# Modulation weights laid out by contraction rows and multiplied on four column groups

## The chip, the cores and the metric

The kernel runs on one core of one Trainium2 chip. The metric is the device time of one execution in microseconds (us). The inputs are float32 throughout, and every matmul is a float32 matmul, which the trace records as two entries (one matmul of 256 moving columns shows as "x2").

## The reference, cut to what matters

One layer of a decoder runs on 256 prompt tokens and 8 sample rows (one new token for each of 8 sequences), at width 1024. The change touches only the modulation: six vectors of 1024 for the prompt and for each of the 8 samples.

```
def adaln(c, w_ada, b_ada):
    m = jax.nn.silu(c) @ w_ada + b_ada
    return [t[:, None, :] for t in jnp.split(m, 6, axis=-1)]

sh1, sc1, g1, sh2, sc2, g2 = adaln(c, w_ada[layer], b_ada[layer])     # for the prompt and for the samples
h  = rms_norm(x, norm_mix) * (1.0 + sc1) + sh1
qa, ka, va, qb, kb, vb = project_qkv(h, w_in, pos)    # 8 stick-breaking heads, 8 dilated window heads
x  = x + g1 * merge_out(oa, ob, norm_out_sb, norm_out_dil, w_out)
h2 = rms_norm(x, norm_ffn) * (1.0 + sc2) + sh2
x  = x + g2 * peer_ffn(h2, ...)                       # 16 of 16384 experts for each of 8 heads
y  = rms_norm(x, norm_final)
```

`w_ada` is 1024 x 6144, `c` has 9 rows (8 samples and the prompt). The samples also attend to 2048 past tokens: paged K and V caches for the stick-breaking heads (16 pages of 128 tokens each), window buffers for the dilated heads. The outputs hold the new K/V rows and whole copies of the window buffers, shifted by one row.

## The kernel before, in words

The kernel is written by hand, engine by engine: each engine has its own program in a fixed order, and semaphores tie them together. Nothing is scheduled automatically. All tiles live in SBUF for the whole run.

Weights come in 48 chunks of 1 MB, four in a round, into four slots (`W`, slots 0 to 3 of `R`). A chunk is 256 output columns of a weight matrix for all 1024 contraction rows, 8 KB on each of 128 partitions. GpSimd (POOL) issues them: the load of a slot's next chunk waits until TensorE (PE) has counted the slot as used (`w_used`). Rounds 0 and 1 are the first two modulation vectors (shift 1, scale 1), rounds 2 to 4 the q/k/v projection, rounds 5 to 8 the other four vectors, round 9 the output projection, rounds 10 and 11 the PEER queries.

The program passes through these stages:

1. Front. `c` is put through silu as 9 rows of 1024 (L815, L1099 to L1101), turned by PE (L461) into `cT`, and multiplied with 8 chunks (`ada_chunk`, L472: eight matmuls with 9 stationary columns and 256 moving columns, then a ninth, L474, that adds the bias by a one-hot selector that ScalarE (ACT) makes, L821). ACT evicts 9x256 pieces to `m_rows` (L827). VectorE (DVE) folds the norm's gain in (L1126), PE spreads the prompt's row over 128 partitions (L481), ACT evicts it to `m_all` (L842), and DVE modulates the three token tiles (L1116, L1117).
2. Projection. PE multiplies 12 chunks (`project`, L510). After the first four it spreads the samples' queries (L532), ACT evicts them, and from there DVE works through the K pages of samples 0 to 3 (`page_scores`: a multiply, L1140, and a reduction, L1142, for each chunk of two pages) beside PE's other eight chunks.
3. Sticks. Four rounds g of a loop, a pair of heads and a sample (4 to 7) each. DVE's order in a round: L1158, K chunks 0 and 1, L1164 and L1166, chunks 2 and 3, L1170, chunks 4 and 5, L1174, chunks 6 and 7, L1177. PE answers between: transposes (L543), scores (L553, L554), sums (L561 to L564), values (L574 to L576), and beside them `ada_chunk` for slots 0 and 1 behind the scores and for slots 2 and 3 behind the sums.
4. V pages of the 8 samples on PE (L594) beside the dilated heads; then the gate's spread (L481) and the V windows of the dilated heads (L699).
5. Output projection (L510), second modulation, PEER queries (L744), and then 264 gathers of expert rows of 1 MB each (L432) with a dot product on DVE and a product on PE for each.

SyncE (SP) issues the other loads in one fixed order. Small inputs come first; then it waits for them (`small_in`) and issues the first 8 K pages (L285); then 24 pieces of 1 MB of the window copies (L296), each held until the piece before it of the same kind has landed; then the K pages of the rest of sample 0 and of samples 1 to 7, each held until DVE has used its slot; then output rows, V pages with some copy pieces between, the V windows (L261, L262: four DMAs for a sample), and the last copies.

Of the kernel before, what the change touches and what calls it, by code (L numbers as in the profile page):

```python
# [15 lines left out]
ALU = mybir.AluOpType  # L16
# [23 lines left out]
NKEY = 128  # L40
NSLOT = 8
# [8 lines left out]
GATE1, SHIFT2, SCALE2, GATE2 = range(4)  # L50
EPS = 1e-6
# [73 lines left out]
def build(nc, A):  # L125
    ctx = ExitStack()
    with ctx:
# [14 lines left out]
        m_rows = sb("m_rows", [9, 4, D])  # L142
# [7 lines left out]
        nffn = sb("nffn", [9, D])  # L150
        b24 = sb("b24", [ADA_CH, WC])
        zd = sb("zd", [P, 3, NB * NH])
        zrow = sb("zrow", [NB * NH, 384])
        pd = sb("pd", [P, 3, NB * NH])
        cT = sb("cT", [P, KC, 9])
        bsel = sb("bsel", [ADA_CH, 2, 9])
# [15 lines left out]
        diag = sb("diag", [P, 4, P])  # L172

# [14 lines left out]
        cwork = [Z[0:9, n, :] for n in range(3)]  # L188
# [15 lines left out]
        def row_slot(k):  # L204
# [18 lines left out]
        names = """c9_in c_in x_in small_in w_used sel_ready ada_mm ada_ev bc_mm bc_ev cs_ready cT_mm cT_ev m1_ready  # L223
# [6 lines left out]
          kst dst sbs dis tks subk_in z_v topsm tope fin_in""".split()  # L230
# [17 lines left out]
        def wait_apart(eng, semaphore, value):  # L248


            if not isinstance(value, int):
                eng.reg_mov(wait_value[eng], value)
                value = wait_value[eng]
            eng.wait_ge(s["c_in"], 48)
            eng.wait_ge(semaphore, value)
# [11 lines left out]
        def _(sp):  # L267
            sp.dma_start(cwork[0], A["c9"]).then_inc(s["c9_in"], 16)
            sp.dma_start(const[:, :], A["consts"]).then_inc(s["c_in"], 16)
            sp.dma_start(cwork[2], A["norm_mix"].to_broadcast([9, D])).then_inc(s["c_in"], 16)  # L270
            sp.dma_start(b24[:, :], A["b_ada"]).then_inc(s["c_in"], 16)
            for t in range(3):
                sp.dma_start(x[0:TP[t], t, :], A["x"][t * P:t * P + TP[t], :]).then_inc(s["x_in"], 16)
            sp.dma_start(nffn[:, :], A["norm_ffn"].to_broadcast([9, D])).then_inc(s["small_in"], 16)
# [3 lines left out]
            sp.wait_ge(s["small_in"], 64)  # L278
# [63 lines left out]

            sp.wait_ge(s["new_out"], 32)
# [109 lines left out]
        def _(pe):  # L453
# [4 lines left out]
            pe.wait_ge(s["c_in"], 48)  # L458
            pe.wait_ge(s["cs_ready"], 1)
            for c in range(KC):  # L460
                last = pe.transpose(ps[:, 7, c * 9:(c + 1) * 9], cwork[0][:, c * P:(c + 1) * P], ident[0:9, 0:9])  # L461
            last.then_inc(s["cT_mm"], 1)
            pe.wait_ge(s["cT_ev"], 1)

            def ada_chunk(r, first, sel, k, bank):

                w_round(r + first, k)

                pe.wait_ge(s["sel_ready"], (r + sel) * WSLOTS + (k + 1))
                out = ps[0:9, bank + k % 2, 0:WC]  # L470
                for c in range(KC):
# [1076 lines left out]
```

## Times and profile before

| | us |
|---|---|
| median of 3 runs | 1369.17 (1368.55 to 1369.77) |
| span of the profiled execution | 1367.5 |
| PE busy in it | 1121.9 (82%) |
| DVE busy | 790.2 (58%) |
| ACT busy | 374.5 (27%) |
| POOL busy | 389.7 (28%) |
| DMA, over the span | 479.79 MB, mean 351 GB/s |

The profiled execution is told by its span, from the first instruction to the last; the median of the unprofiled runs is 1.7 us above it. Busy shares are averages over stages with different limits, so what counts for an edit is the stage that it stands in and which engine or transfer is the last to be ready there. The profile's chain of waits follows the work back from the last instruction, and its waits view says for whom each engine sat idle.

### The profile page before, as it was taken

Reading aid. Unit: us, or ns where it says so; the run is one execution under the profiler, and the core shown is the slowest. Engines: PE = TensorE matmul, PEld = TensorE weight load, DVE = VectorE, ACT = ScalarE, POOL = GpSimd, SP = SyncE. Lnnn points to the kernel's source line nnn. Section 1 sums busy time; section 2 is a strip of 40 time slices with the busy share of each in tenths; the row PEclk is TensorE's granted clock in tenths of the full one; section 3 lists DMA queues with packets and bytes.
Section 4 is the critical chain, followed back from the end, with each engine's and each line's share of the span. In section 5 each row is a group of like instructions: output and inputs, shape, how many; then the busy total and the mean of one; then the engine's idle time right before and its main releaser. Section 6 shows DMA issues by size and latency. Waiting matters only on the chain.

```text
span 1367.5 us, 14726 instructions
## 1 busy us (share of the span) xinstructions
PE 1121.9 (82%) x3386; PEld 503.3 (37%) x3386; DVE 790.2 (58%) x1679; ACT 374.5 (27%) x1030; POOL 389.7 (28%) x384
## 2 busy tenths in 40 slices
PE   6799998998787888998997778777768777777875
PEld 2375774443221211457852323233223333232321
DVE  4203996976512411324437777777777677777755
ACT  1201004434110000002233333333344334444323
POOL 1000003020201000000125555555535555555540
PEclk9898999996999997998999999999999999999998
DMA  9998887898698886899659999999999999999995
GB/s 335 426 358 303 298 312 270 323 356 301 220 284 252 251 269 215 322 390 339 232 207 423 422 422 422 422 422 422 422 421 379 422 422 422 422 422 422 422 422 221
DMA packets 91422, 479.79 MB, mean 351 GB/s; under 512 B 11792, under 2 KB 11817, under 8 KB 50172
## 3 DMA queue, kind: packets, MB, share of 16 engines
q0 software_dynamic: 46912, 332.47, 60.3%
q1 hardware_dynamic: 44476, 146.92, 30.9%
q8 instruction: 15, 0.25, 0.1%
q14 instruction: 19, 0.16, 0.0%
HBM read 476.10 MB, written 70.32 MB: 400 GB/s over the span
## 4 chain that ended last, share of the span: by engine, by line
PE 37%; DMA 32%; issue 10%; DVE 8%; SPq 6%; ACT 4%; POOL 2%; POOLq 0%; DVEq 0%; ACTq 0%
DMA R<-in_uv,idst 26%; PE ps L510 13%; PE ps L791 8%; PE ps L744 4%; SPq L284 3%; DMA R<-in_sb_v 3%; PE ps L472 3%; SPq L285 2%; DVE R L1140 2%; PE ps L699 2%; PE ps L594 2%; POOL R L432 2%; DMA R<-in_sb_k 2%; PE ps L481 1%; ACT wgt L1050 1%
## 5 line engine op out<-in xcount | busy, mean ns | idle before, releaser
L791 PE MATMUL ps<-R,diag 128*128 128x512 f32 x1024 | 482.1, 619 | 153.4 <-ACT diag L1069 153.4
L432 POOL DMA_INDIRECT R<-in_uv,idst x256 | 320.9, 1254 | 332.5 <-PE ps L791 260.4
L1454 DVE CUSTOM_DVE_ANT_0 R<-R,H 128x1024 f32<-128x1024 f32 x264 | 318.6, 1222 | 162.7 <-DMA R<-in_uv,idst 152.3
L791 PEld LDWEIGHTS ps<-R,diag 128*128 128x128 f32 x1024 | 192.4, 196 | 443.1 <-ACT diag L1069 241.6
L510 PE MATMUL ps<-R,HT 128*128 128x256 f32 (+1 forms) x768 | 172.7, 384 | 1.0 <-DVE HT L1335 0.4
L378 POOL DMA_DIRECT2D R<-in_wts x44 | 23.4, 531 | 508.9 <-PE ps L510 341.9
L594 PE MATMUL ps<-R,ast 128*8 128x512 f32 x256 | 123.0, 625 | 27.6 <-DMA R<-in_sb_v 24.0
L510 PEld LDWEIGHTS ps<-R,HT 128*128 128x128 f32 (+1 forms) x768 | 119.0, 158 | 55.3 <-issue 12.1
L1047 ACT ACTIVATE gel<-dots 128x2 f32<-128x2 f32 x132 | 26.8, 203 | 377.3 <-DVE dots L1454 377.3
L1140 DVE TENSOR_TENSOR R<-R 128x1024 f32<-128x1024 f32 x64 | 78.2, 1221 | 66.2 <-ACT R L874 57.6
L472 PE MATMUL ps<-R,cT 128*9 128x256 f32 x384 | 92.8, 398 | 1.3 <-ACT bsel L821 1.3
L1069 ACT ACTIVATE diag<-const,wgt 128x128 f32<-128x128 f32 x256 | 89.1, 394 | 16.1 <-PE ps L791 3.2
L1142 DVE TENSOR_REDUCE Z<-R 128x1024 f32 x64 | 78.1, 1220 | 9.1 <-DVE R L1140 0.2
L1258 DVE TENSOR_TENSOR msk<-ps,const 8x512 f32<-8x512 f32 x16 | 10.9, 679 | 97.4 <-PE ps L594 57.5
L594 PEld LDWEIGHTS ps<-R,ast 128*8 128x8 f32 x256 | 20.8, 92 | 119.6 <-issue 67.9
L1050 ACT ACTIVATE wgt<-gel,gst 128x1 f32<-128x1 f32 x264 | 63.3, 287 | 4.3
L744 PE MATMUL ps<-HT,R 128*128 128x264 f32 x256 | 59.9, 393 | 0.3 <-ACT HT L855 0.3
L472 PEld LDWEIGHTS ps<-R,cT 128*9 128x9 f32 x384 | 34.3, 94 | 55.8 <-issue 14.8
L744 PEld LDWEIGHTS ps<-HT,R 128*128 128x128 f32 x256 | 49.0, 194 | 8.6 <-ACT HT L855 0.4
L863 ACT ACTIVATE QKV<-ps 128x512 f32 (+1 forms) x12 | 7.2, 598 | 120.9 <-PE ps L510 120.9
L261 POOL DMA_DIRECT2D m_all<-in_dil_k x24 | 12.9, 538 | 95.6 <-DVE zd L1223 95.0
L699 PE MATMUL ps<-R,ast 128*8 128x512 f32 (+2 forms) x48 | 29.8, 775 | 7.9 <-DMA R<-out_dil_v_s 5.8
(233 smaller groups left out, 872.3 us busy)
## 6 DMA issues: line engine op xcount, KB each, us to landing
R<-in_wts POOLq DMA_DIRECT2D x48, 1024.0 KB, 8.1
R<-in_sb_k SPq DMA_DIRECT2D x128, 256.0 KB, 4.4
R<-in_sb_v SPq DMA_DIRECT2D x128, 256.0 KB, 3.4
out_dil_k_s<-in_dil_k SPq DMA_DIRECT2D x32, 1023.5 KB, 8.0
out_dil_v_s<-in_dil_v SPq DMA_DIRECT2D x32, 1023.5 KB, 7.9
R<-in_uv,idst POOLq DMA_INDIRECT x256, 12.1
m_all<-in_dil_k POOLq DMA_DIRECT2D x16, 192.0 KB, 6.1
R<-in_dil_v SPq DMA_DIRECT2D x16, 192.0 KB
```

The source lines that it names most:

```text
L432: pool.indirect_dma_start(out=R[:, row_slot(k), :], out_offset=None, in_=A["uv"], in_offset=bass.IndirectOffsetOnAxis(ap=idst[:, par, k:k ...
L472: last = pe.matmul(out, cT[:, c, :], W[k][:, c, :], start=(c == 0), stop=False)
L510: last = pe.matmul(out, hT[:, c, t * P:t * P + TP[t]], W[k][:, c, :], start=(c == 0), stop=(c == KC - 1))
L594: last = pe.matmul(ps[0:NH, 6 + j, :], ast[:, j, c * KVP + g, :], KV[c % KVS][:, g, :], start=(c + g == 0), stop=(c * KVP + g == NPG - 1))
L699: last = pe.matmul(ps[0:NH, 6 + j, :], ast[0:n, j, g, :], DV[j][0:n, g, :], start=(g == 0), stop=(g == 2))
L744: last = pe.matmul(ps[:, j, 0:NTOK], W[k][:, c, j * P:(j + 1) * P], hT[:, c, :], start=(c == 0), stop=(c == KC - 1))
L791: last = pe.matmul(ps[:, banks + q, :], diag[:, k % 4, :], R[:, row_slot(k), D + q * 512:D + (q + 1) * 512], start=False, stop=False, skip ...
L1050: last = act.activation(wgt[:, k + q:k + q + 1], gel[:, k + q:k + q + 1], ACT.Copy, scale=gst[:, k + q:k + q + 1])
L1069: act.activation(diag[:, k % 4, :], ident, ACT.Copy, scale=wgt[:, k:k + 1]).then_inc(s["diag_done"], 1)
L1140: kc.inc(dve.tensor_tensor(kv, kv, q, ALU.mult))
L1142: dve.tensor_reduce(z4[:, c * KVP:(c + 1) * KVP, bass.ds(b, 1), :].rearrange("p g a h -> p g (a h)"), kv.rearrange("p g (h d) -> p g h d", ...
L1454: dve.tensor_tensor_reduce(u, u, H[:, t, :], 1.0, 0.0, ALU.mult, ALU.add, dots[:, k:k + 1]).then_inc(s["dot_done"], 1)
```

## The change

The modulation weights are laid out in another way in memory: a chunk now holds 256 of the 1024 contraction rows for one whole vector of 1024 columns (`pairs` in place of `chunks`), so a round of four chunks is one vector. A chunk is still 1 MB, 8 KB on each partition. PE multiplies a chunk with two contraction blocks and four column blocks of 256: the output of column block q goes to partitions 32q to 32q+8 of one PSUM bank, with 32 stationary columns (9 of `c` and 23 of zeros) on column group q of the array. `c` comes already turned (`cT`, 128 x 8 x 32). The bias matmul, its selector and ACT's evictions go. The bias, laid out on the same partitions (`mq`), is added by DVE as it evicts the bank (`ada_rows`). The samples' rows, which must be on partitions 0 to 7 for tile 2, are moved from `mq` to `m_rows` by DMAs of 8 x 1 KB: 8 from ACT's queue in the front, 16 from SP's in front of the V windows. The prompt's row is spread by matmuls over all 128 contraction rows, 256 columns at a time.

```diff
-            sp.dma_start(cwork[0], A["c9"]).then_inc(s["c9_in"], 16)
+            sp.dma_start(cT[:, :, :], A["cT"].rearrange("p (c n) -> p c n", c=KC)).then_inc(s["c9_in"], 16)
             sp.dma_start(const[:, :], A["consts"]).then_inc(s["c_in"], 16)
-            sp.dma_start(cwork[2], A["norm_mix"].to_broadcast([9, D])).then_inc(s["c_in"], 16)
-            sp.dma_start(b24[:, :], A["b_ada"]).then_inc(s["c_in"], 16)
             for t in range(3):
                 sp.dma_start(x[0:TP[t], t, :], A["x"][t * P:t * P + TP[t], :]).then_inc(s["x_in"], 16)
-            sp.dma_start(nffn[:, :], A["norm_ffn"].to_broadcast([9, D])).then_inc(s["small_in"], 16)
+            sp.wait_ge(s["mq_clear"], 1)
+            for k in range(QUADS):
+                q = slice(k * QUAD, k * QUAD + NB + 1)
+                cols = slice(k * WC, (k + 1) * WC)
+                sp.dma_start(mq[q, :, :], A["b_ada"][k:k + 1].to_broadcast([NB + 1, VECTORS, WC])).then_inc(s["mq_in"], 16)
+                sp.dma_start(nq[q, 0, :], A["norm_mix"][:, cols].to_broadcast([NB + 1, WC])).then_inc(s["mq_in"], 16)
+                sp.dma_start(nq[q, 1, :], A["norm_ffn"][:, cols].to_broadcast([NB + 1, WC])).then_inc(s["mq_in"], 16)
...
             value_pages(NB - 1)
 
+            sp.wait_ge(s["m2_ready"], 1)
+            for v, slot in LATE_VECTORS:
+                for k in range(QUADS):
+                    sp.dma_start(m_rows[:, slot, k * WC:(k + 1) * WC], mq[k * QUAD:k * QUAD + NB, v, :]).then_inc(s["mr_in"], 16)
             sp.wait_ge(s["new_out"], 32)
...
-            def ada_chunk(r, first, sel, k, bank):
-                w_round(r + first, k)
-                pe.wait_ge(s["sel_ready"], (r + sel) * WSLOTS + (k + 1))
-                out = ps[0:9, bank + k % 2, 0:WC]
-                for c in range(KC):
-                    last = pe.matmul(out, cT[:, c, :], W[k][:, c, :], start=(c == 0), stop=False)
-                last.then_inc(s["w_used"], 1)
-                pe.matmul(out, bsel[:, k % 2, :], b24[:, :], start=False, stop=True).then_inc(s["ada_mm"], 1)
+            def ada_slots(r, first, bank, slots):
+                for k in slots:
+                    w_round(r + first, k)
+                    for c in range(2):
+                        for q in range(QUADS):
+                            last = pe.matmul(ps[q * QUAD:(q + 1) * QUAD, bank, 0:WC], cT[:, 2 * k + c, :],
+                                             WA[k][:, c, q * WC:(q + 1) * WC], start=(k + c == 0), stop=(2 * k + c == KC - 1))
+                    last.then_inc(s["w_used"], 1)
...
-                for k in range(2):
-                    ada_chunk(g, 5, 2, k, 6)
+                if not first:
+                    pe.wait_ge(s["ada_ev"], g + 2)
+                ada_slots(g, 5, 6, (0, 1))
...
+            act.wait_ge(s["m1_ready"], 1)
+            for v, slot in FIRST_VECTORS:
+                for k in range(QUADS):
+                    act.dma_start(m_rows[:, slot, k * WC:(k + 1) * WC], mq[k * QUAD:k * QUAD + NB, v, :]).then_inc(s["mr_in"], 16)
...
+            dve.memset(mq[:, :, :], 0.0)
+            dve.memset(nq[:, :, :], 0.0).then_inc(s["mq_clear"], 1)
...
+            def ada_rows(v, bank, chunks_used):
+                dve.wait_ge(s["w_used"], chunks_used)
+                mv = mq[:, bass.ds(v, 1), :].rearrange("p a n -> p (a n)")
+                dve.tensor_tensor(mv, ps[:, bank, 0:WC], mv, ALU.add).then_inc(s["ada_ev"], 1)
...
                 page_scores(g + 4, (6, 7))
+                ada_rows(g + 2, 6, g * WSLOTS + (2 * WSLOTS + QKV_CH + WSLOTS))
                 dve.wait_ge(s["o_mm"], g + 1)
...
+    def pairs(w):
+        return w.reshape(WSLOTS, 2, P, -1, D).transpose(3, 0, 2, 1, 4).reshape(-1, P, 2 * D)
```

Three places show how the instructions stand. On PE, in the first round of the sticks stage, behind the second score matmul (`ps<-R,cT` are the modulation's, `ps<-b,bsel` the bias's), before:

```order
49 L554 MATMUL ps<-HT 128x128
50 L472 MATMUL ps<-R,cT 9x256 x8
51 L474 MATMUL ps<-b,bsel 9x256
52 L472 MATMUL ps<-R,cT 9x256 x8
53 L474 MATMUL ps<-b,bsel 9x256
54 L561 MATMUL ps<-H,const 128x128
```

The same place after:

```order
33 L566 MATMUL ps<-HT 128x128
34 L481 MATMUL ps<-R,cT 32x256 x16
35 L574 MATMUL ps<-H,const 128x128
```

Two chunks are 16 matmuls in both; their outputs are 32 partitions instead of 9, and the two bias matmuls between are gone. On DVE, at the end of a round of the sticks loop, behind the last K chunk, before and then after:

```order
104 L1142 ISA
105 L1142 TENSOR_REDUCE Z<-R 128x2x8
106 L1177 ISA
107 L1177 COPY QKV<-ps 128x2x128
108 L1155 REGISTER_ALU
```

```order
108 L1147 TENSOR_REDUCE Z<-R 128x2x8
109 L1100 ISA
110 L1102 ISA
111 L1102 TENSOR_TENSOR mq<-ps,mq 128x256
112 L1183 ISA
113 L1183 COPY QKV<-ps 128x2x128
```

One more operation, and the wait of L1100 for PE's four slots, stand in front of the copy of the values. On SP, between the last V page and the first V windows, before and then after:

```order
508 L285 DMA R<-in_sb_v 128x512
509 L261 DMA R<-in_dil_v 128x512
510 L261 DMA R<-in_dil_v 96x512 x2
511 L262 DMA R<-out_dil_v_s 1x512
```

```order
517 L295 DMA R<-in_sb_v 128x512
518 L356 DMA m_rows<-mq 8x256 x16
519 L267 DMA R<-in_dil_v 128x512
520 L267 DMA R<-in_dil_v 96x512 x2
521 L268 DMA R<-out_dil_v_s 1x512
```

Sixteen small DMAs now stand in front of the V windows of samples 0 and 1.

## Rows read from the trace of the kernel before

**Rows 1.** The page: the chain that ended last, by engine.
```profile
PE 37%; DMA 32%; issue 10%; DVE 8%; SPq 6%; ACT 4%; POOL 2%; POOLq 0%; DVEq 0%; ACTq 0%
```
**Rows 2.** Windows by stage: PE, PEld, DVE, ACT, POOL busy, granted clock, DMA share, GB/s.
```profile
0.00:122.50 122.50, 101.00 (x393) 52.72 (x393) 22.64 (x20) 20.60 (x47) 8.86 (x20) 0.90 0.97 372
122.50:214.30 91.80, 88.86 (x398) 61.40 (x398) 75.73 (x64) 10.49 (x23) 7.41 (x16) 0.98 0.85 286
214.30:320.00 105.70, 93.82 (x446) 45.37 (x446) 94.34 (x97) 37.85 (x70) 20.28 (x37) 0.89 0.91 325
```
**Rows 3.** Timeline of the front: start, us, engine, line.
```profile
14.13 5.09 PE L472 MATMUL ps<-R,cT 128*9 128x256 f32 x16 [0.60 <-ACT bsel L821]
27.83 3.62 PE L472 MATMUL ps<-R,cT 128*9 128x256 f32 x16
48.42 0.59 PE L474 MATMUL ps<-b,bsel 24*9 24x256 f32 x2
66.96 42.69 PE L510 MATMUL ps<-R,HT 128*128 128x256 f32 x192 [0.31 <-ACT HT L855]
```
**Rows 4.** SP's timeline: first K pages, last of 24 copies, next pages.
```profile
23.09 8.10 SPq L285 DMA_DIRECT2D R<-in_sb_k  x8
122.37 0.51 SPq L296 DMA_DIRECT2D out_dil_v_s<-in_dil_v  x1
126.88 183.68 SPq L285 DMA_DIRECT2D R<-in_sb_k  x120
```
**Rows 5.** DMA queues (packets, MB, share): 70 to 80 us, then 80 to 90 us.
```profile
q1 hardware_dynamic: 93, 3.01, 85.8%
...
q1 hardware_dynamic: 77, 2.23, 53.5%
q0 software_dynamic: 143, 1.05, 26.8%
```
**Rows 6.** DVE's timeline: first and fifth K chunk, last of sample 3, sticks begin.
```profile
123.52 1.22 DVE L1140 TENSOR_TENSOR R<-R 128x1024 f32<-128x1024 f32 x1 [57.60 <-ACT R L874]
133.51 1.21 DVE L1140 TENSOR_TENSOR R<-R 128x1024 f32<-128x1024 f32 x1
204.59 1.22 DVE L1142 TENSOR_REDUCE Z<-R 128x1024 f32 x1
214.35 1.14 DVE L1158 TENSOR_SCALAR H<-ps,sbb 128x384 f32<-128x384 f32 x2 [8.54 <-PE ps L554]
```
**Rows 7.** Waits of DVE, 215 to 320 us: us, times, longest.
```profile
DVE R L1140 <- DMA R<-in_sb_k: 6.5, 4, 3.2
```
**Rows 8.** DVE's timeline in a sticks round: an operation that reads PSUM.
```profile
264.84 0.41 DVE L1177 COPY QKV<-ps 128x256 f32 x1
```
**Rows 9.** PE's timeline at the sticks' start: scores on 64 rows.
```profile
213.24 0.71 PE L553 MATMUL ps<-HT 64*128 64x256 f32 x4 [1.19 <-ACT HT L887]
213.78 0.40 PE L554 MATMUL ps<-HT 64*128 64x128 f32 x4
```
**Rows 10.** Groups of weight loads: L472 from 0 to 70 us, L510 (page); busy, mean ns.
```profile
L472 PEld LDWEIGHTS ps<-R,cT 128*9 128x9 f32 x128 | 11.3, 93 | 19.6 <-issue 4.2 <-ACT bsel L821 2.3
...
L510 PEld LDWEIGHTS ps<-R,HT 128*128 128x128 f32 (+1 forms) x768 | 119.0, 158 | 55.3 <-issue 12.1
```
**Rows 11.** SP and PE at the V windows.
```profile
508.00 1.29 SPq L261 DMA_DIRECT2D R<-in_dil_v  x3
516.29 8.29 PE L699 MATMUL ps<-R,ast 128*8 128x512 f32 x12 [0.47 <-ACT selst L921]
523.35 0.23 SPq L262 DMA_DIRECT2D R<-out_dil_v_s  x1
526.12 2.74 PE L699 MATMUL ps<-R,ast 128*8 128x512 f32 x6 [0.58 <-DMA R<-out_dil_v_s]
```
**Rows 12.** SP's issue of one DMA, in ns (min/median/max): from memory, from 8 partitions.
```profile
L261 SPq DMA_DIRECT2D R<-in_dil_v x24: 317/352/556, 508.0 to 551.8; - x24
L324 SPq DMA_DIRECT2D out_sb_k_n<-QKV x1: 1452/1452/1452, 315.8 to 315.8; - x1
```

More of the change, by code:

```diff
@@ L40 @@
 NKEY = 128
+QUAD = 32
+QUADS = P // QUAD
+VECTORS = 6
+PROMPT = NB
 NSLOT = 8
@@ L186, in build @@
         z1, zt, zl = Z[:, 0, :], Z[:, 1, :], Z[:, 2, :]
-        cwork = [Z[0:9, n, :] for n in range(3)]
+        cwork = [Z[:, n, 0:KC * QUAD] for n in range(2)]
+        WA = [R[:, s, :].rearrange("p (c n) -> p c n", c=2) for s in range(WSLOTS)]
         Hf = H[:, :, :].rearrange("p t n -> p (t n)")
@@ L455, in w_round @@
                 pe.wait_ge(w_ready[k], r * 16 + 16)
[L458 removed]
+            pe.wait_ge(s["c_in"], 16)
             pe.wait_ge(s["cs_ready"], 1)
[L460 to L474 removed]
@@ L476, in spread_rows @@
-            def spread_rows(order, n, banks, mm, ev):
-                for m, slot in enumerate(q for q in order for _ in range(2)):
+            def ada_slots(r, first, bank, slots):
[6 more added lines that the diff above has]
+                    last.then_inc(s["w_used"], 1)
@@ L479, in spread_rows @@
+            def spread_rows(vectors, n, banks, mm, ev):
+                for m, v in enumerate(v for v, _ in vectors for _ in range(2)):
                     if m >= len(banks):
                         pe.wait_ge(ev, n + m - len(banks) + 1)
-                    pe.matmul(ps[:, banks[m % len(banks)], :], ident[0:9, 8:9].to_broadcast([9, P]),
-                              m_rows[:, slot, (m % 2) * 512:(m % 2 + 1) * 512], start=True, stop=True).then_inc(mm, 1)
+                    for j in range(2):
+                        k = 2 * (m % 2) + j
+                        last = pe.matmul(ps[:, banks[m % len(banks)], j * WC:(j + 1) * WC],
+                                         ident[:, k * QUAD + PROMPT:k * QUAD + PROMPT + 1].to_broadcast([P, P]),
+                                         mq[:, v, :], start=True, stop=True)
+                    last.then_inc(mm, 1)
@@ L513, in project @@
                         last.then_inc(s["w_used"], 1)
-            with pe.Fori(0, 2) as r:
-                for k in range(WSLOTS):
-                    ada_chunk(r, 0, 0, k, 0)
+            for r in range(2):
+                ada_slots(r, 0, r, range(WSLOTS))
             pe.wait_ge(s["m1_ready"], 1)
-            spread_rows((SHIFT1, SCALE1), 0, (4, 5, 6, 7), s["bc_mm"], s["bc_ev"])
+            spread_rows(FIRST_VECTORS, 0, (4, 5, 6, 7), s["bc_mm"], s["bc_ev"])
             pe.wait_ge(s["bc_ev"], 4)
@@ L565, in sticks_pair @@
                 last.then_inc(s["s_mm"], 1)
-                for k in range(2, 4):
-                    ada_chunk(g, 5, 2, k, 6)
+                ada_slots(g, 5, 6, (2, 3))
                 pe.wait_ge(s["s_am"], g + 1)
@@ L1529 @@
         "pages": a["page_table"].reshape(1, NB * NPG),
-        "wts": np.concatenate([chunks(w) for w in (a["w_ada"][0][:, :2 * D], a["w_in"][0], a["w_ada"][0][:, 2 * D:],
-                                                   a["w_out"][0], a["w_peer_q"][0])], 0),
+        "wts": np.concatenate([pairs(a["w_ada"][0][:, :2 * D]), chunks(a["w_in"][0]), pairs(a["w_ada"][0][:, 2 * D:]),
+                               chunks(a["w_out"][0]), chunks(a["w_peer_q"][0])], 0),
         "subk": a["peer_sub_keys"].reshape(16, NKEY, P).transpose(2, 0, 1).reshape(P, 16 * NKEY),
```

99 lines of the change are left out of this document (43 added, 56 removed).

## The prediction, made before the changed kernel was run

> **What bounds the kernel now.** I read the chain that ended last first [rows 1]: no engine holds it, PE has 37% of it and DMA 32%, so the kernel must be read by stages. The windows [rows 2] give three that the change touches. The front and the first chunks of the projection, up to 122.5 us, keep PE busy for 101.0 us with the DMA engines at a share of 0.97. From 122.5 to 214.3 us PE is busy for 88.9 of 91.8 us beside DVE's K pages of samples 0 to 3. In the sticks stage, 214.3 to 320.0 us, PE shows 93.8 us and DVE 94.3 us of 105.7: both look full, and only the waits tell which is last.
>
> They say this. In the sticks stage DVE waits for K pages, 6.5 us in all [rows 7], and in a list of what it waited for there PE does not stand. So DVE and its pages set that stage, and PE's modulation matmuls lie beside it. One wait for PE stands just ahead of it: DVE ends sample 3's pages at 204.59 + 1.22 = 205.8 us and then idles 8.54 us until the first scores, at 214.35 us [rows 6], because PE is still in the projection. And SP shows a limit that the chain hides [rows 4]: the 24 copy pieces end at 122.37 + 0.51 = 122.9 us, and only behind them come the pages from the fifth chunk on, at 126.88 us, 3.1 us after DVE began at 123.52 us. Before the change that limit is just covered.
>
> **The front.** The eight modulation chunks run from 14.13 us to 48.42 + 0.59 = 49.0 us [rows 3], 34.9 us. A chunk is 16 entries in 3.62 us less the overlap of the last, 0.222 us each, the first at half clock. A chunk of the new layout has the same 16 entries of 256 columns. If four column groups ran fully side by side, a chunk would take 0.9 us; PE would then wait for the weights. The trace shows tiles overlapping only for row groups: two score matmuls of 256 columns and two of 128, on 64 rows each, run from 213.24 to 214.18 us [rows 9], 0.94 us, where one after the other at 0.222 us for an entry of 256 columns they need 2 x 0.44 + 2 x 0.22 = 1.33 us. I take it that column groups overlap as well, and that the chunks then come at the pace of their loads: the second four MB are asked for by about 18 us instead of 20 to 32 us, and at some 0.35 MB per us beside the K pages they are in by about 30 to 33 us. That is 16 to 19 us earlier than 49.0; the two evictions on DVE stand for ACT's last one. The bounds are 34.9 - 28.4 = 6.5 us (no overlap: 128 entries x 0.222 = 28.4 us) and about 20 us. The silu is on 256 elements a partition rather than 1024, and the 8 DMAs on ACT's queue stand ahead of its evictions; both fall into the same term. The projection, 192 entries in 42.69 us for its first four chunks [rows 3], keeps its length, so the first scores, at 213.24 us now [rows 9], could stand about 17 us earlier, near 196 us.
>
> **What is late next.** DVE's pages of samples 0 to 3 could start near 106 us, but their fifth chunk cannot: SP still has copies to issue. How far do these move? Copies alone run at 3.0 MB in 10 us, and at 2.2 MB beside 1.05 MB of weights [rows 5]: one MB of weights costs them 0.8 MB, some 2.6 us. With PE 17 us ahead, 1 to 2 more chunks (one for 10.65 us) fall into their time: +2.5 to 5 us. The front's DMA is denser earlier, -2. The first K pages stand behind 12 small DMAs more, +0 to 2. I take +2.5, so the copies are issued by 125.4 us. The fifth chunk needs two pages to be issued (about 1 us each, 8 in 8.10 us [rows 4]) and some 5 us to land: 132.4 us, against 133.51 us before [rows 6]. DVE's last page of sample 3 then ends at 204.7 us and, since PE is ready at 196 us, the sticks begin there: 214.35 - 204.8 = 9.5 us earlier. The front's large term is cut to this, the idle 8.54 us and 1 us more. PE's other 8 us gained end as waiting for DVE. Bounds of this term: 12.5 us (copies not later) and 3.5 us (copies and landings 6 us later still).
>
> **The sticks stage.** Removed from PE are four chunks of 4.1 us (3.55 us and a bias matmul) of its 93.82 / 4 = 23.5 us a round, 16.3 us; put in at a quarter to seven eighths of that: worth nothing, as DVE is last there. Added on DVE are four evictions of 128x256 with an addition, each like the copy of 256 columns from PSUM, 0.41 us [rows 8]: 4 x 0.4 = +1.6 us. Behind each stand the copy of the values and the next round's first operation, for which ACT and PE wait in turn. The added wait on `w_used` is over long before: the slots of a round are multiplied behind L561 to L564, 13 us ahead of it. PE will be idle more and may run at the half level of the clock; the granted clock fell to 0.89 of full over this stage already [rows 2]. Between DVE's last mask (L1174) and its next L1158 lie two K chunks (32 in 82.3 us [rows 6], 2.6 us each) and the copy, 5.5 us, in which PE and ACT must do values, transposes and scores; at half clock I estimate 6 for them, so up to 0.5 us for each of three rounds and a little at the end: +1 us, between 0 and 3. The waits for pages, 6.5 us [rows 7], can move: weights are asked for in pairs at once, but 2 MB of them ahead of the stage. I keep them at 6.5, between 0 and 10.
>
> **The V windows.** SP issues 16 small DMAs ahead of the windows. The price of one issue is 0.35 us for loads from memory and was 1.45 us for one from 8 partitions of SBUF [rows 12], which stood in a stretch where SP's other issues were slow too. I take 0.35: 5.6 us, and keep 16 x 1.45 = 23.2 us as the other end. Sample 0's windows are four issues (1.29 us for three, 1.9 in all) and landed within 2.5 us of the last where the queue was empty: 523.35 + 0.23 to 526.12 us [rows 11]. Moved by 5.6 us they are there at 508.0 + 5.6 + 1.9 + 2.5 = 518.0 us, and PE wanted them at 516.29 us: +2 us (bounds 0 and 19). The later windows wait for PE's use and follow it. The last copies start later by the same, but end 50 us ahead of the gathers. The gate's spread is the same number of columns, in twice the entries of half the width: 0.
>
> **The sum.** -9.5 + 1.6 + 1 + 2 = -4.9 us. Everything behind is tied to these stages by waits and moves with them, the gathers at their pace. The span of 1367.5 becomes 1362.6; the median of the runs lies 1.7 us above the span, so 1369.2 - 4.9 = 1364.3 us.
>
> The Trainium skill speaks against the layout at one place: by "TensorE: Matmul & The Clock Gate", Part 3 (packing small matmuls), a weight load overlaps a running matmul only where their row groups differ, and here all four column groups use all rows. This trace doesn't agree for full-width matmuls: entries with loads of 93 ns and entries with loads of up to 190 ns (158 ns in the mean) [rows 10] both follow each other at 0.222 us (192 in 42.69 us [rows 3]), so the load is hidden. The same part gives 2.38 times for three column tiles, which would make the front's PE work about 12 us, an estimate by that page; the loads cover it either way.
>
> **The rivals.**
> - No overlap of column groups. For it: no row shows it for columns. Against: the row groups. PE ends 6.5 us earlier, the sticks start at 207.9 us: -6.5 + 1.6 + 2 = -2.9, 1366.3 us.
> - No overlap and the weight loads in the open. An entry costs 0.222 + 0.093 = 0.315 us, the front 40.3 us (+5.4), a sticks round 64 x 0.315 + 7.2 = 27.4 us of PE against 26.4 (+4), windows +2: 1380 us. It is the page's rule as a mechanism; rows 10 speak against it.
> - The small DMAs in front of the V windows (the slower side). At 1.45 us an issue the windows are there at 508.0 + 23.2 + 1.9 + 2.5 = 535.6 us, +19.3 instead of +2: 1381.6 us. It eats the whole gain where an issue costs over 0.65 us (16 t = 6.9 + 8.3 - 4.4 = 10.8 us).
> - The copies hold DVE. If the fifth chunk comes at 138.5 us, the sticks begin near 210.9 us: -3.5 + 4.6 = +1, 1370.3 us: the front's gain is hidden anyway.
> - The copies aren't later, or the page waits of the sticks go: -3 or -6.5 more, near 1358 us.
>
> **How the numbers follow.** Forecast 0.47, with a range of its own of 1361 to 1367; no overlap 0.12; loads in the open 0.04; slow small issues 0.10; copies hold DVE 0.15; better 0.12. A change of 0.2% (2.7 us) is about what a measurement of this kernel can tell from none. Faster by more: nearly all of the forecast, half of no overlap, all of better: 0.62. Within: 0.22. Slower: slow issues, loads in the open, and the bad part of the copies: 0.16. The range is 1357 to 1371: it takes in the better case and the copies, and leaves out the two cases near 1380.
>
> **What would show it.** The first L523 starts near 48 us (66.96 before); copies are issued by 125 us; the fifth K chunk at 132 us with a wait for its page; the wait of 8.54 us for PE is gone and the first score evictions stand near 205 us; PE idle in the sticks stage, DVE not; the first V window matmul waits for its DMA, 2 us late. I am wrong if the sticks begin later than 208 us, if they take over 110 us, or if the windows start over 5 us late against the last V page.

## The result

The kernel after takes 1381.89 us in the median of 18 runs (1371.33 to 1388.60), the kernel before 1370.29 us in 18 runs on the same chips (1363.34 to 1378.38). The ratio is 1.0082 (95% interval 1.0061 to 1.0102): the change makes the kernel slower by 11.6 us, where 4.9 us faster was forecast. The profiled execution has a span of 1380.5 us against 1367.5, 13.0 us more.

### The profile page after: what moved, and what is told of

It reads as the page before. It is cut to its first block, busy times and chain, and to the rows that moved or that the text cites. A ratio compares the mean times of both kernels' runs of the same rounds, so it can differ in the third digit from the quotient of the medians.

```text
span 1380.5 us, 14581 instructions
## 1 busy us (share of the span) xinstructions
PE 1057.9 (77%) x3354; PEld 495.3 (36%) x3354; DVE 788.1 (57%) x1687; ACT 363.4 (26%) x979; POOL 396.1 (29%) x384
## 4 chain that ended last, share of the span: by engine, by line
DMA 42%; PE 24%; issue 11%; SPq 9%; DVE 7%; ACT 4%; POOL 2%; POOLq 0%; DVEq 0%; ACTq 0%
DMA R<-in_uv,idst 25%; PE ps L803 8%; DMA out_dil_v_s<-in_dil_v 6%; DMA R<-in_sb_k 5%; PE ps L756 4%; SPq L294 4%; PE ps L606 3%; PE ps L523 3%; SPq L295 3%; DMA R<-in_sb_v 2%; POOL R L446 2%; DVE R L1145 2%; DMA pages<-in_pages 2%; PE ps L711 1%; DVE R L1460 1%
## 5 line engine op out<-in xcount | busy, mean ns | idle before, releaser
L446 POOL DMA_INDIRECT R<-in_uv,idst x256 | 325.4, 1271 | 328.5 <-PE ps L803 256.7
L1061 ACT ACTIVATE diag<-const,wgt 128x128 f32<-128x128 f32 x256 | 89.5, 395 | 17.1 <-PE ps L803 4.2
L481 PE MATMUL ps<-R,cT 128*32 128x256 f32 x384 | 36.4, 534 | 24.0 <-DMA R<-in_wts 21.6
L574 PE MATMUL ps<-H,const 128*128 128x128 f32 x16 | 5.7, 461 | 38.9 <-DVE H L1171 38.9
## 6 DMA issues: line engine op xcount, KB each, us to landing
R<-in_uv,idst POOLq DMA_INDIRECT x256, 12.2
```

Source lines behind the costliest of these rows:

```text
L446: pool.indirect_dma_start(out=R[:, row_slot(k), :], out_offset=None, in_=A["uv"], in_offset=bass.IndirectOffsetOnAxis(ap=idst[:, par, k:k ...
L1061: act.activation(diag[:, k % 4, :], ident, ACT.Copy, scale=wgt[:, k:k + 1]).then_inc(s["diag_done"], 1)
```

## The profile after

The chain that ended last, by engine, answers [rows 1]: DMA has 42% of it instead of 32%, PE 24% instead of 37%.

```profile
DMA 42%; PE 24%; issue 11%; SPq 9%; DVE 7%; ACT 4%; POOL 2%; POOLq 0%; DVEq 0%; ACTq 0%
```

The three stages that answer [rows 2] (the same columns: us, then PE, PEld, DVE, ACT, POOL busy, granted clock, DMA share, GB/s):

```profile
0.00:112.00 112.00, 80.31 (x378) 47.64 (x379) 18.58 (x24) 16.03 (x29) 8.89 (x20) 0.91 0.96 355
112.00:219.40 107.40, 89.69 (x428) 61.51 (x426) 77.29 (x64) 9.95 (x23) 17.87 (x30) 0.93 0.86 301
219.40:327.40 108.00, 55.35 (x384) 39.85 (x384) 95.14 (x101) 31.17 (x38) 11.65 (x22) 0.64 0.91 321
```

The front is 10 us shorter than before, the second stage 15.6 us longer, and the third 2.3 us longer though PE is busy in it for 55.35 us instead of 93.82. So PE lost work, and the time went into something else. PE's timeline of the front, against [rows 3]:

```profile
10.94 1.93 PE L481 MATMUL ps<-R,cT 128*32 128x256 f32 x16 [10.94 <-DMA R<-in_wts]
...
35.11 1.57 PE L481 MATMUL ps<-R,cT 128*32 128x256 f32 x16 [0.48 <-DMA R<-in_wts]
37.70 3.72 PE L492 MATMUL ps<-mq,const 128*128 128x256 f32 x16 [1.02 <-DVE mq L1133]
...
54.51 15.81 PE L523 MATMUL ps<-R,HT 128*128 128x256 f32 x58 [0.31 <-ACT HT L852]
```

All eight modulation chunks wait for their weights, each takes 1.93 us (the last 1.57 us) instead of 3.62, and the last ends at 35.11 + 1.57 = 36.7 us instead of 49.0: 12.3 us earlier. (The first four loads take until 23.77 us to land, so POOL asks for the last of the second four at 26.39 us.) The projection starts at 54.51 us instead of 66.96, 12.5 us earlier. Between the two stands ACT, which issues 8 small DMAs before its first eviction (ACTq is ACT's queue):

```profile
37.68 5.88 ACTq L841 DMA_DIRECT2D m_rows<-mq  x8
43.60 2.06 ACT L835 ACTIVATE m_all<-ps 128x512 f32<-128x512 f32 x4 [23.12 <-issue]
```

SP's timeline answers [rows 4], and DVE's [rows 6]:

```profile
8.88 0.28 SPq L287 DMA_DIRECT2D pages<-in_pages  x1
34.38 8.12 SPq L295 DMA_DIRECT2D R<-in_sb_k  x8
42.55 0.66 SPq L306 DMA_DIRECT2D out_dil_k_s<-in_dil_k  x1
```

```profile
134.56 0.51 SPq L306 DMA_DIRECT2D out_dil_v_s<-in_dil_v  x1
135.89 14.12 SPq L295 DMA_DIRECT2D R<-in_sb_k  x9
```

```profile
112.38 1.23 DVE L1145 TENSOR_TENSOR R<-R 128x1024 f32<-128x1024 f32 x1 [59.26 <-ACT R L871]
...
121.24 1.22 DVE L1147 TENSOR_REDUCE Z<-R 128x1024 f32 x1
146.22 1.23 DVE L1145 TENSOR_TENSOR R<-R 128x1024 f32<-128x1024 f32 x1 [23.76 <-DMA R<-in_sb_k]
...
219.41 1.14 DVE L1163 TENSOR_SCALAR H<-ps,sbb 128x384 f32<-128x384 f32 x2
```

DVE begins 11.1 us earlier (112.38 us against 123.52), works through the four chunks that it has, and then idles 23.76 us for the fifth, which comes at 146.22 us instead of 133.51. SP could not issue it: the 24 copy pieces end 12.2 us later than before. The sticks start at 219.41 us, 5.1 us later instead of 9.5 us earlier. The wait of 8.54 us for PE ahead of them is gone. PE starts its first scores at 201.84 us, against 213.24 us [rows 9]: 11.4 us of its gain arrive here, and DVE is not ready to use them.

```profile
201.84 0.71 PE L565 MATMUL ps<-HT 64*128 64x256 f32 x4 [1.19 <-ACT HT L884]
```

The DMA queues show what stands behind the late copies (packets, MB, share of the 16 engines; q0 carries the weights, q1 is SP's). First the kernel after from 20 to 30 us, then from 30 to 40, then from 50 to 60:

```profile
q0 software_dynamic: 431, 3.14, 94.4%
q1 hardware_dynamic: 280, 0.17, 7.3%
```

```profile
q0 software_dynamic: 536, 3.88, 93.8%
q1 hardware_dynamic: 207, 0.26, 7.2%
```

```profile
q1 hardware_dynamic: 151, 3.80, 99.9%
```

Before, from 30 to 40 us:

```profile
q1 hardware_dynamic: 810, 3.40, 84.6%
q0 software_dynamic: 182, 1.35, 32.2%
```

The new layout uses a slot in 1.93 us, so POOL asks for weights nearly as fast as they land, and up to 40 us they take most of the engines' time. In the ten microseconds from 30 us SP's queue moved 0.26 MB, against 3.40 MB before. This is not contention alone: SP still waited for the page table and issued its first K page at 34.38 us. Then PE's slow chunks of the projection (10.65 us each) ask for little: from 37.9 to 68.6 us POOL issues no weight chunk, and from 50 to 70 us the copies run nearly alone.

Two things can be counted. By the issue of the 24th copy, at 122.37 us, the kernel before had moved 45.5 MB, 28.75 of them on SP's queue and 16.77 of weights: 372 GB/s. The kernel after had moved 47.0 MB (29.10 and 17.81) at 134.56 us: 350 GB/s. So 1.5 MB more stood ahead of that point, mostly one more weight chunk, and the pace was lower. At the pace before, the 1.5 MB are some 4 us (an estimate from these numbers), and the lower pace is the other 8 of the 12.2 us. The lower pace stands mostly in one stretch: the totals up to 30 us and from 70 to 120 us differ by under 0.2 MB each, from 30 to 70 us the two queues moved 17.1 MB before and 14.8 MB after.

In the sticks stage DVE's waits answer [rows 7] (us, times, longest):

```profile
DVE R L1145 <- DMA R<-in_sb_k: 7.4, 6, 2.5
DVE H L1163 <- PE ps L566: 0.7, 1, 0.7
```

The stage lasts from 219.41 to 327.40 us, 108.0 us against 105.6: four `ada_rows` at 0.416 us, 0.9 us more waiting for pages, 0.7 us for PE. One profile doesn't fix such a difference: the same stage took 107.9 to 113.1 us in the kernels below with this layout, and 111.4 us in the second run of e7's kernel, which has the old one. In front of the V windows, against [rows 11], SP and then PE:

```profile
520.77 10.89 SPq L356 DMA_DIRECT2D m_rows<-mq  x16
531.78 1.31 SPq L267 DMA_DIRECT2D R<-in_dil_v  x3
```

```profile
524.82 1.99 PE L492 MATMUL ps<-mq,const 128*128 128x256 f32 x8
...
536.53 7.70 PE L711 MATMUL ps<-R,ast 128*8 128x512 f32 x12 [8.77 <-DMA R<-out_dil_v_s]
```

The 16 small DMAs take 10.89 us, 0.68 us each. The first window matmul comes 11.7 us behind the gate's spread (524.82 to 536.53), before it came 3.5 us behind it (512.79 to 516.29): +8.2 us.

The 13.0 us by stages: start of the sticks +5.1; sticks +2.4; from there to the gate's spread +4.6; windows' start +8.2; and then -3.7 to the merge, -2.0 to the second modulation, -1.8 to the first gathered dot product, +0.3 behind it. The +4.6 can't be put down to the layout: in the kernels below with this layout, that stretch lasts between 190.6 and 199.6 us, and in three profiles with the old one 192.8 (before), 193.3 and 195.9 us.

## The experiments

e1 to e4 ran on one chip, e6 to e9 on a second and e10 to e12 on a third, each time beside the kernel before (1372.02, 1372.73 and 1371.72 us there). Where runs from two chips are compared, the ratios to the kernel before count.

Two theories stood for the late copies. One: the page table (`pages`) is issued behind 12 small loads, at 8.88 us instead of 5.31, so SP reads it late and everything behind it slips. The other: weights asked for earlier take the transfer engines from the copies, wherever the page table stands.

**The small loads first (e1_small_first).**

```diff
+            sp.dma_start(sbb...); sp.dma_start(gcol...); sp.dma_start(pages...)      # small_in
             sp.wait_ge(s["mq_clear"], 1)
             for k in range(QUADS):
                 ...                                                                  # the 12 loads of mq and nq
-            sp.dma_start(sbb...); sp.dma_start(gcol...); sp.dma_start(pages...)
             sp.wait_ge(s["small_in"], 48)
```

> The changed kernel with SP's three last small loads (stick bias, output gain, page table) issued ahead of the 12 small loads of biases and norm gains instead of behind them. Theory (late page table: K pages, copies and with them the fifth K chunk are late because the page table's load lands at 33.4 us behind the 12 new small loads): SP's first K page near 22 us instead of 34.4, last copy issued near 124 us instead of 134.6, fifth K chunk near 135 us instead of 146.2, time about 11 us under the changed kernel, ratio to the kernel before near 1.000. Rival (the copies are late because earlier weight loads take their bandwidth, wherever they start): last copy issued after 130 us, time within 4 us of the changed kernel.

1382.87 us (5 runs), ratio 1.008 (1.0048 to 1.0111): as slow as the kernel after. SP's timeline, and DVE's:

```profile
25.86 8.14 SPq L295 DMA_DIRECT2D R<-in_sb_k  x8
34.06 0.66 SPq L306 DMA_DIRECT2D out_dil_k_s<-in_dil_k  x1
```

```profile
131.97 0.51 SPq L306 DMA_DIRECT2D out_dil_v_s<-in_dil_v  x1
```

```profile
141.17 1.23 DVE L1145 TENSOR_TENSOR R<-R 128x1024 f32<-128x1024 f32 x1 [16.85 <-DMA R<-in_sb_k]
```

SP's first pages and copies come 8.5 us earlier than in the kernel after, the last of the 24 only 2.6 us. The copies now take 98 us instead of 92. The fifth chunk comes 5 us earlier, but later pages are waited for more, and the sticks start at 218.51 us, 0.9 us earlier. The first theory falls as an explanation of the time; it is true only of when the copies start. (This profile is of the slowest of the five executions.)

**The page table before the second round of weights (e4_hold_weights).**

```diff
+            pool.wait_ge(s["small_in"], 48)
             weight_rounds(1, 6)
```

> The changed kernel with POOL's second round of modulation weights held until the small loads have landed. Theory A (small packets are slow on SP's queue because POOL's queue always has 8 KB packets beside them): page table landed by about 24 us instead of 33.4, copies issued by 126 us, time 7 to 10 us under the changed kernel although the modulation ends some 6 us later. Theory B (the 12 small loads take their time by themselves): page table still after 30 us, time within 3 us of the changed kernel.

1385.21 us (4 runs), ratio 1.0094 (1.0062 to 1.0125). Its SP:

```profile
26.65 8.09 SPq L295 DMA_DIRECT2D R<-in_sb_k  x8
```

```profile
133.11 0.51 SPq L306 DMA_DIRECT2D out_dil_v_s<-in_dil_v  x1
```

The page table is read 7.7 us earlier with nothing moved on SP, so the weights beside it had held it up. The 24th copy still goes out at 133.11 us, and DVE's first chunk is later too (121.18 us, 112.38 in the kernel after). The expected gain of 7 to 10 us did not come. A start of the copies some 8 us earlier moved their end by 2.6 us in e1 and by 1.4 us here, and the pace up to the 24th copy was 349 and 346 GB/s, no higher than in the kernel after.

**The 16 row DMAs behind the windows (e2_rows_late), and both moves (e3_both).**

```diff
-            sp.wait_ge(s["m2_ready"], 1)
-            for v, slot in LATE_VECTORS: ...                 # 16 DMAs mq -> m_rows
             ...
             for b in range(2):
                 window_rows(sp, DV, b, b, A["dil_v"], A["dil_v_s"], dv_ready)
+            sp.wait_ge(s["m2_ready"], 1)
+            for v, slot in LATE_VECTORS: ...
```

> The changed kernel with the 16 small DMAs of the sample rows moved on SP from in front of the V windows of samples 0 and 1 to behind them, where SP waits for PE anyway. Theory (the issue of 16 DMAs, 10.9 us, holds the V windows): the first window matmul stands 3 to 4 us behind the gate's spread instead of 11.7 us, time about 8 us under the changed kernel, ratio near 1.002. Rival (the windows would be late anyway, by their own landing): first window matmul still over 8 us behind, time within 3 us of the changed kernel.

1378.01 us (10 runs), ratio 1.0042 (1.0014 to 1.0071). PE at the windows:

```profile
521.48 1.99 PE L492 MATMUL ps<-mq,const 128*128 128x256 f32 x8
...
524.89 5.33 PE L711 MATMUL ps<-R,ast 128*8 128x512 f32 x12 [0.47 <-ACT selst L913]
```

The wait of 8.77 us for the windows is gone, and 3.4 us lie between the spread and the first window matmul, as before. The next two samples' windows now stand behind the 16 DMAs and PE waits 5.23 us for them, so a part of the 8.3 us is given back: the ratio falls by 0.4%, some 5 us (the two intervals just overlap).

> Both moves at once. If the two causes are separate and all of the loss, the gains add: some 19 us under the changed kernel, ratio to the kernel before near 0.995. If the second K-page stall or PE's lower clock in the sticks stage is a cause of its own, the ratio stays at 1.000 or above.

1377.73 us, ratio 1.0052 (1.0027 to 1.0078): the small loads add nothing to e2, as e1 says, and the 19 us that I expected of both moves came to about 4. The copies end at 135.04 us and the fifth chunk comes at 146.35. It is the base of the next three.

**Eight copy pieces out of the front (e6_copies_later).** On top of e3:

```diff
                     copy_windows(0, 0)
                     copy_windows(0, 1)
-                    copy_windows(1, 0)
...
-                        copy_piece(2, 0, c // 4, q)          # beside the V pages
+                        copy_piece(1, 0, c // 4, q)
...
-            for pair, odd in ((2, 1), (3, 0), (3, 1)):       # at the end
+            for pair, odd in ((2, 0), (2, 1), (3, 0), (3, 1)):
```

> The kernel of e3 (small loads first, sample rows late) with 8 of the 24 copy pieces moved out of the front: sample 2's pieces take the places among the V pages, sample 4's go to the end with the last copies. Theory (the copies in front of the fifth K chunk are the place where the front's gain is lost): the last of 16 pieces is issued near 100 us, DVE's wait at the fifth chunk shrinks from 21.8 us to under 3 us, sticks end near 312 us instead of 329, time about 15 us under e3, ratio to the kernel before near 0.992. Rival (DMA bandwidth as a whole holds the K pages of the first three stages, whoever asks first): the wait is spread over the later K pages, sticks end above 322 us, ratio above 1.000.

1364.84 us, ratio 0.9945 (0.9918 to 0.9972): 1.1% below e3's ratio, some 14 us, and faster than the kernel before. SP, then the end of DVE's pages of sample 3 and its start of the sticks:

```profile
102.02 0.51 SPq L306 DMA_DIRECT2D out_dil_v_s<-in_dil_v  x1
117.72 6.40 SPq L295 DMA_DIRECT2D R<-in_sb_k  x6
```

```profile
195.71 1.22 DVE L1146 TENSOR_REDUCE Z<-R 128x1024 f32 x1
206.45 1.14 DVE L1162 TENSOR_SCALAR H<-ps,sbb 128x384 f32<-128x384 f32 x2 [9.51 <-PE ps L565]
```

The last of 16 pieces goes out at 102.02 us. The next K pages are held until 117.72 us by DVE's own use of the slots. No wait for a page in the projection is over 1.1 us, and the sticks start at 206.45 us behind a wait of 9.51 us for PE. So the copies were what held DVE. That 206.45 us lies near the 204.8 us of the prediction is in part luck: there PE was ready at 196 us and DVE's pages ended last, at 204.7 us; here DVE's pages end at 196.9 us and PE is last, with its first scores at 204.61 us. The sticks end at 314.9 us, near the 312 expected and far from the rival's 322.

**The same move in the kernel before (e7_before_copies_later).** Its diff is the one above, on the kernel before.

> The kernel before, with the same 8 copy pieces moved out of the front and nothing else. Theory (before the change PE's projection covers the copies, so they cost nothing there): first K chunk still at 123.5 us, sticks end within 4 us of 320 us, ratio 0.997 to 1.003. Rival (the copies cost the kernel before as much): sticks end below 312 us, ratio under 0.993.

1367.42 us, ratio 0.9965 (0.9935 to 0.9995). A gain may be there (the forecast had been 0.997 to 1.003), but it is small: the copies were nearly covered before. Its profiled execution had DVE begin late (129.97 us), so only the times say it.

**Weights one at a time (e8_paced).** On top of e3, each chunk of rounds 1 and 2 is asked for when the one before it has landed:

```diff
-            weight_rounds(1, 6)
+            for n in range(WSLOTS, 3 * WSLOTS):
+                m = n - 1
+                pool.wait_ge(s["w_used"], n - WSLOTS + 1)
+                pool.wait_ge(w_ready[m % WSLOTS], 16 * (m // WSLOTS + 1))
+                pool.dma_start(R[:, n % WSLOTS, :], A["wts"][n]).then_inc(w_ready[n % WSLOTS], 16)
+            weight_rounds(3, 6)
```

> The kernel of e3 with the weight chunks of rounds 1 and 2 asked for one at a time, each after the one before it has landed. Theory (weights in a burst shut SP's queue out up to 50 us, and then copies, two in flight, do not fill the DMA engines: the overlap of the two is lost): SP's queue moves over 1.5 MB in each 10 us from 30 us on instead of 0.7, the 24th copy is issued near 124 us instead of 135, sticks end near 319 us, time about 9 us under e3, ratio near 0.998. Rival (the total of bytes sets the copies' end): 24th copy still after 130 us, time within 3 us of e3.

1395.52 us, ratio 1.0177 (1.0121 to 1.0232): 17.8 us above e3, where 9 us below it was expected. The queues from 50 to 70 us, SP's last of 24 copies, and what PE waited for from 0 to 150 us:

```profile
q1 hardware_dynamic: 169, 5.70, 77.5%
q0 software_dynamic: 146, 1.07, 13.9%
```

```profile
121.50 0.51 SPq L306 DMA_DIRECT2D out_dil_v_s<-in_dil_v  x1
```

```profile
PE ps L486 <- DMA R<-in_wts: 49.7, 8, 12.6
```

The copies end at 121.50 us, as the theory had it, but now the weights lose. A chunk of 1 MB asked for beside the copies takes 13 to 15 us to land, much as in the kernel after (14.1 us in the median of five from 60 to 130 us). With only one under way that becomes the pace of the front: PE waits 49.7 us for weights instead of 21.6, the projection starts at 86.31 us and DVE begins at 146.63 us.

The run doesn't decide between its theory and its rival. By the 24th copy the queues had moved 42.7 MB here (13.5 of weights, 352 GB/s) and 46.9 MB in e3 (17.7 of weights, 347 GB/s). At e3's pace the 4.1 MB that were not moved are some 12 of the 13.5 us by which the copies end earlier (an estimate). That weights came all along, instead of in a burst, raised the pace hardly at all.

Nor can a rule for sharing be read from the 169 packets of copies and 146 of weights in these 20 us. In the two microseconds from 52 us the weights moved 48 packets, 0.39 MB, and SP's queue 15 packets of under 0.01 MB; of the chunk asked for at 49.19 us 0.93 MB had moved by 58 us, and it landed at 63.2 us. A stretch in which both queues have work all the time is that from 10 to 20 us. In the kernel after:

```profile
q0 software_dynamic: 368, 2.66, 81.0%
q1 hardware_dynamic: 356, 0.81, 21.4%
```

The Trainium skill says that an engine goes round its queues packet by packet ("DMA: Bandwidth & Descriptors", Queues, rings and completion order). The trace agrees here: 368 and 356 packets, and before the change 391 and 383. Bytes then go by the size of a packet, 7 KB against 2.3 KB. In the ten microseconds from 20 us it is 431 packets against 280 (3.14 against 0.17 MB), no longer equal. So the small loads and the page table get few bytes beside a burst of weights, as e4 found.

**Four pieces in flight (e9_four_in_flight).** On top of e3, the pieces of samples 0 and 1 are issued in turn, so that four are under way instead of two:

```diff
-                    copy_windows(0, 0)
-                    copy_windows(0, 1)
+                    for q in range(4):
+                        for odd in range(2):
+                            for m in range(2):
+                                copy_piece(0, odd, m, q)
                     copy_windows(1, 0)
```

> The kernel of e3 with the copies of samples 0 and 1 interleaved, so that four pieces of 1 MB are in flight instead of two. Theory (alone, two pieces in flight move 3.0 to 3.3 MB in 10 us, where weights and copies together move 4.1): SP's queue near 4 MB in 10 us from 50 to 70 us, the 24th copy issued near 125 us instead of 135, time about 8 us under e3. Rival (a copy is bound by the engines or the memory, not by how many are in flight): each piece takes twice as long, 24th copy after 131 us, time within 3 us of e3.

1372.86 us, ratio 1.0016 (0.9983 to 1.0048), 4.9 us below e3 where 8 were expected (the two intervals overlap). SP, DVE, and SP's queue from 50 to 70 us:

```profile
127.51 0.51 SPq L306 DMA_DIRECT2D out_dil_v_s<-in_dil_v  x1
```

```profile
137.78 1.22 DVE L1147 TENSOR_TENSOR R<-R 128x1024 f32<-128x1024 f32 x1 [13.25 <-DMA R<-in_sb_k]
```

```profile
q1 hardware_dynamic: 349, 7.51, 108.7%
```

Four in flight move 7.51 MB in these 20 us, two in flight moved 6.05 MB in e3 and 6.69 in the kernel after. The copies end 7.5 us earlier than in e3 with nearly the same bytes moved (46.0 and 46.9 MB), 361 GB/s against 347, and the sticks start at 211.75 us instead of 219.48. So copies with two in flight leave the engines partly idle when they run alone. That this is the pace lost in the kernel after fits the stretch from 50 to 70 us, but no run shows that it is all of it.

**Both, and the two layouts once more side by side (e10, e11, e12, on one chip).** e10 is e6 with four pieces in flight, e11 is e6 again, e12 is e7 again.

> The kernel after with the page table and the small DMAs moved and 8 copy pieces taken out of the front (as e6_copies_later), and the 16 copies that stay interleaved over samples 0 and 1, so that up to four are in flight. Theory (copies alone with two in flight do not fill the transfer engines, and they hold DVE's pages): the 16 copies end near 110 us instead of 117.7; but in e6 the next K pages were already there before DVE wanted the fifth chunk (waits of about 1 us), so the sticks still start when PE is ready, near 206 us, and the time stays within 0.3% of e6: ratio to before 0.992 to 0.997. Rival (the front still pays for the copies through slower weights or landings): PE's projection comes earlier or later with them and the ratio differs from e6's by over 0.4%.

> The kernel of e6_copies_later once more, to be compared on one chip with e12. Theory: with the copies out of the way the new layout is worth what PE gains in the front less the later costs of DVE and PE (some 4 to 8 us): ratio to before 0.992 to 0.997. Rival (all of e6's gain is the moved copies, the layout gives nothing): the ratio is that of e12, within 0.2%.

> The kernel of e7_before_copies_later once more: the old layout with 8 copy pieces moved. Theory: the copies were just covered in the kernel before, so moving them is worth 0 to 0.3%: ratio 0.997 to 1.000, and PE (modulation, then projection) sets the sticks' start at 213 to 222 us. Rival: ratio as e11's, 0.992 to 0.997.

e10: 1362.80 us, ratio 0.9949 (0.9926 to 0.9973). e11: 1364.25 us, 0.9954 (0.9930 to 0.9978). e12: 1371.30 us, 1.0003 (0.9980 to 1.0027). The last copy piece of e10's front, then its sticks' start, and that of e12:

```profile
92.08 0.51 SPq L306 DMA_DIRECT2D out_dil_v_s<-in_dil_v  x1
```

```profile
203.56 1.14 DVE L1164 TENSOR_SCALAR H<-ps,sbb 128x384 f32<-128x384 f32 x2 [4.39 <-PE ps L567]
```

```profile
214.83 1.14 DVE L1157 TENSOR_SCALAR H<-ps,sbb 128x384 f32<-128x384 f32 x2 [5.46 <-PE ps L553]
```

In e10 the copies are out 10 us earlier than in e6 (92.08 us; I had expected the 16th near 110 us, having taken e6's 117.72 us, the issue of the next pages, for the end of its copies) and the time is that of e6: with the pages waiting for DVE, faster copies buy nothing. e11 against e12 is the new layout against the old with the copies out of the way; e11 also has the page table first and the sample rows' DMAs behind the windows, two moves of loads that only the new layout has. There the layout is worth 7.0 us (1364.25 against 1371.30; the intervals of the two ratios just part). The pair e6 and e7 on the other chip gives 2.6 us, with intervals that overlap. Over both pairs (23 runs of e6 and e11, 22 of e7 and e12) the medians are 1364.2 and 1369.0 us, 4.8 us or 0.4% for the new layout. In the profiles both kernels wait for PE at the sticks, and e11 starts them 8.1 us earlier than e12 (206.70 and 214.83 us); its span is 7.9 us shorter. The best version is e10 or e6, which can't be told apart.

## Why the prediction was wrong, step by step

| step | predicted | measured |
|---|---|---|
| start of the sticks | -9.5 | +5.1 |
| sticks stage (`ada_rows`, clock, pages) | +2.6 | +2.4 |
| V stage | 0 | +4.6 (190.6 to 199.6 us with these instructions) |
| start of the V windows | +2 | +8.2 |
| windows to the end | 0 | -7.2 |
| sum | -4.9 | +13.0 |

- **What is late next: the step that failed.** I saw that the copies would bound DVE and let them slip by 2.5 us, the sum of +2.5 to 5 us for one or two more weight chunks among them, -2 for "the front's DMA is denser earlier" and 0 to 2 for the K pages behind 12 small loads. They slipped by 12.2 us. The first part was right in kind: 1.5 MB more had moved by the 24th copy, some 4 us. The -2 had the wrong sign: the pace of the transfers fell from 372 to 350 GB/s, some 8 us, most of it between 30 and 70 us. The price of 0.8 MB of copies for each MB of weights was read where both were under way together; it has no place for copies that start late behind a burst of weights and then run alone. e6 shows that the copies held DVE: with 8 pieces fewer the stage starts at 206.45 us. e1 and e4 show that an earlier start of the copies does not cure it; e9 shows that more of them in flight cures part. Why the pace fell is argued from e9 and the queues, and not shown by a run of its own. The rival "the copies hold DVE" was this, with the fifth chunk at 138.5 us; it came at 146.22.
- **The small DMAs in front of the windows: the second term that was mis-sized.** I chose 0.35 us for an issue, the price of loads from memory, though the nearest row of a DMA out of SBUF was 1.45 us [rows 12]. It was 0.68 us, which made the term +8.2 us instead of +2. The text gave 0.65 us as the point where the gain is eaten; its own sum, 10.8 / 16, is 0.675. e2 shows that the place costs some 5 us of the total. The two rivals of the slower side came true together, the copies beyond their price (+5.1 us at the sticks' start instead of -3.5), the small DMAs at part of theirs (8.2 of 19.3 us).
- **The front.** Right in kind: the column groups overlap and the chunks wait for their loads. In size 12.3 us instead of 16 to 19, because the second four MB were asked for by 26.4 us and not by 18: each load waits for its slot's use, and the first four landed only by 23.8 us. The projection began at 54.51 us, not near 48; of that up to 3.6 us are ACT's 8 DMAs: PE has filled the last bank at 37.70 + 3.72 = 41.4 us, and an eviction of 0.6 us behind it would end at 42.0 us instead of 43.60 + 2.06 = 45.7. I had put them into a term without a price. No run took them away.
- **No overlap, and weight loads in the open.** Both fell: 16 entries in 1.57 to 1.93 us are 0.10 to 0.12 us an entry, less than the 0.222 us of one alone, and their weight loads of 32 columns (158 ns in the mean in the front) run under matmuls: 16 of them one after the other would need 2.5 us. Full overlap of the four groups would be 0.9 us a chunk; whether the loads are a part of the rest was not tried. The rule of the Trainium skill that a load overlaps only where the row groups differ ("TensorE: Matmul & The Clock Gate", Part 3) is not seen here. The 2.38 times that the same part of the Trainium skill gives is for three column tiles; four gave 3.62 / 1.57 = 2.3 in the last chunk.
- **The sticks stage.** Right in its mechanism: DVE bounds it, PE's lost work (93.82 to 55.35 us busy) buys nothing, an `ada_rows` costs 0.416 us, and the mean granted clock fell from 0.89 to 0.64 of full, between the levels of 1.2 and 2.4 GHz, at a price of 0.7 us of waiting for PE. Page waits were 7.4 us for the 6.5 kept. That the sum came out at +2.4 for +2.6 is in part luck, since kernels with these instructions spread over 5 us in this stage (page waits of 11.4 us in e2).
- **Behind.** That all later work moves along was wrong by 7 us: the window loop, the output projection and the queries took back part of the delay. Why each gave what it gave was not tried.
- **A reading.** SP's next K pages are issued 126.88 - 123.52 = 3.4 us behind DVE's start, not 3.1; no term rests on it.

What stays open: why the transfers were slower from 30 to 70 us, the V stage, which lasted 190.6 to 199.6 us in kernels with the same instructions, and the front's DMAs on ACT's queue.

## What to carry to other kernels

An engine that gets faster asks for its loads earlier: before pricing what it gains, list who else uses the transfer engines in that stretch, and what they will run beside instead. Count what had moved by the point that matters, and at what pace: that tells more bytes from slower ones, and an experiment that changes both decides nothing. If a transfer of little urgency stands in a fixed queue ahead of an urgent one, move it before speeding up anything in front of it. A small DMA costs its issue on the queue of whoever issues it, so it belongs behind the loads that somebody waits for.

## What the runs showed of the hardware

- Matmuls on four column groups with 32 stationary columns overlap in float32: 16 entries of 256 columns in 1.57 to 1.94 us, against 3.62 us one after the other.
- With work on both queues from 10 to 20 us, they moved nearly the same number of packets (368 and 356 in the kernel after, 391 and 383 before) and bytes by their size: 2.66 MB of weights against 0.81 MB of small loads. From 20 to 30 us it was 431 and 280 packets, 3.14 and 0.17 MB.
- A weight chunk of 1 MB asked for beside two copies took 13 to 15 us to land in e8.
- Copies from memory to memory, 1 MB each, moved 6.05 MB in 20 us (e3) and 6.69 MB (kernel after) with two in flight and 7.51 MB with four (e9).
- Issuing a DMA of 8 x 1 KB from SBUF to SBUF took 0.68 us on SP and 0.73 us on ACT's queue, twice the 0.35 us of a load from memory.
